# The gate projection of the first block: from 24 plain weight panels to 42 half-size block products

## The chip, the cores and the metric

One core of a Trainium2 chip runs the whole program. The metric is the device time of one execution in microseconds; each kernel is run several times and the median is quoted. The engines are TensorE (PE, matmuls, with its weight loads as PEld), VectorE (DVE), ScalarE (ACT), GpSimd (POOL) and SyncE (SP, which issues most of the DMA transfers). They run side by side, each through its own list of instructions in order, and meet at semaphores.

## The reference

The program computes two transformer blocks on 512 tokens of 1024 features, in fp32. The change touches only the gates of the first block:

```
h = rmsnorm(x, attn_norm_g[l])
z = h @ w_in[l]
gates = jax.nn.sigmoid(h @ w_gate[l] + b_gate[l])
...
merged = g_a * (y_a @ proj_a[l]) + g_b * (y_b @ proj_b[l]) + g_c * (y_c @ proj_c[l])
x = x + merged @ w_out[l]
```

`w_gate` is 1024 x 3072, so the gates are one product of 512 x 1024 by 1024 x 3072. Beside it stands the attention of four heads, `y_c`: for each head two score matrices of 512 x 512 (causal), a softmax of each, their difference, and the product with the values. The gates are first used when the branches `y_a`, `y_b`, `y_c` are projected and merged.

## The kernel before, in words

Activations lie feature by feature: a tile of 128 features by 512 tokens. Every fp32 product is made of three matmuls (`three`): the high part of the weights by the high part of x, high by low, low by high. A **panel** is 128 x 1024 weights, that is, all eight 128 x 128 blocks that one tile of 128 output features needs; it costs 24 matmuls of 512 columns. Panels come by a ring of four: SP loads one into `stage` (a place is free again when DVE has made the low part of the panel four earlier), ACT copies it into the high part `wh` (`hi`; it waits for the load, and for PE to have finished the panel four earlier), DVE subtracts to the low part `wl` (`lo`), and PE multiplies (`features`), then raises `panel_done`.

The order of work is written out by hand for each engine. The stages around the change: u, va, pool (18 panels are numbered up to the gates, `P_GATE` = 18), then eight panels of queries and keys (`P_Q`), the spatial and pool products, four panels of values (`P_V`), then 24 gate panels, then `P_PROJ`, `P_WOUT` and the feed-forward `P_UP`.

The first 16 gate panels are spread over the four heads, four to a head, in a hardware loop `Fori(0, 4)`. In one head PE does: gate panel 0; scores of query blocks 0 and 1; panel 1 with scores 2 and 3 in its middle; panel 2; panel 3 with the transposes of the softmax (`turn`) between its parts; then the product with the values (`values`). DVE takes each gate panel from PSUM and scales it by the row norm (`evac_row` into `tmp`), takes bias and maximum of the score blocks (`score_pair`, L1486), blends the two softmaxes (L1523 to L1532), and makes low parts. ACT makes the high parts, the tanh of the gates, the exponentials (`exp_pair`) and the high part of the transposed softmax. The last eight gate panels stand beside the norms of the four head outputs: sums of squares (`head_sums`, `turn_heads`), a power on POOL, a row spread over the partitions (`head_row`), and the high and low parts of `yc`, on which the projection waits (`yc_ready`).

POOL is nearly idle here. Later, in the two feed-forwards, the same seven-product scheme is already in use: sums of weight blocks are made by DMA transfers that add into SBUF (`add_first1`, L1964, and `add_third1`, L1971), and by DVE.

Of the kernel before, what the change touches and what calls it, by code (L numbers as in the profile page):

```python
# [54 lines left out]
P_U, P_VA, P_POOL, P_Q, P_K, P_V, P_GATE, P_PROJ, P_WOUT, P_UP = 0, 2, 4, 6, 10, 14, 18, 42, 50, 58  # L55
# [223 lines left out]
def semaphores(nc):  # L279
# [457 lines left out]
def sync_program(nc, sp, s, b, dram, scratch, out):  # L737
# [46 lines left out]
    for row in range(P_UP // RING * RING, P_UP):  # L784
        load_row(row, row - RING)
# [44 lines left out]
    for u in range(RING):  # L830
        sp.dma_start(b.stage[:, (start + u) % RING, :], stream[start + u]).then_inc(s.load[(start + u) % RING], 16)
# [59 lines left out]
def scalar_program(nc, act, s, b, dram, scratch, line_dram, out):  # L891
# [97 lines left out]
    def gate(g, half, dst, evac):  # L989
        act.wait_ge(s.evac, evac + 1)  # L990
        bias = b.half_bg[:, g:g + 1] if isinstance(g, int) else b.half_bg[:, bass.ds(g, 1)]
        AR(dst, b.tmp[:, half, :], ACT.Tanh, bias=bias, scale=0.5).then_inc(s.gated, 1)
# [8 lines left out]
    with act.Fori(0, 4) as i:  # L1001

        act.dma_start(b.bias[:], bias_tile(scratch, i)).then_inc(s.bias_in, 16)
        act.wait_ge(s.evac, E_K + 4)
        AR(b.qh[:], b.qk[:, i, :], ACT.Copy, scale=0.125).then_inc(s.qk_hi, 1)
        AR(b.kh[:], b.qk[:, 4 + i, :], ACT.Copy).then_inc(s.qk_hi, 1)
        act.wait_ge(s.evac, E_V + 4)
        AR(b.vh[:], b.v[:, :, bass.ds(P * i, P)], ACT.Copy).then_inc(s.v_hi, 1)
        for u in range(4):
            hi(Panel(P_GATE + u + RING, RING, i))  # L1010
            if u != 2:
                gate(4 * i + u, u % 2, b.ga[:, 4 * i + u, :], E_GATE + 4 * i + u)
            if u == 0:
                for qb in range(TT):
                    act.wait_ge(s.negated, 4 * i + qb + 1)
                    exp_pair(qb)
            if u == 2:
                for kb in range(TT):
                    if kb == 2:
                        gate(4 * i + u, u % 2, b.ga[:, 4 * i + u, :], E_GATE + 4 * i + u)  # L1020
                    act.wait_ge(s.turned, 4 * i + kb + 1)
                    w = (TT - kb) * P
                    A(b.th[:, turned_offset(kb):turned_offset(kb) + w], b.ps[:, 5 + kb % 2, 0:w],
                      ACT.Copy).then_inc(s.turned_hi, 1)

        act.wait_ge(s.scored, 8 * i + 8)
        act.wait_ge(s.score_done, 8 * i + 8)
        act.wait_ge(s.pv_done, i + 1)


    act.wait_ge(s.pv_done, 4)
    for pair in range(2):
# [6 lines left out]
    for u in range(8):  # L1039
        hi(Panel(P_GATE + 16 + u + RING))  # L1040
        gate(16 + u, u % 2, b.gatec[:, u, :], E_GATE + 16 + u)
        if u == 0:
            act.wait_ge(s.ocol_done, 1)
            A(b.osum[0:4, :], b.ps[0:4, 7, :], ACT.Copy).then_inc(s.o_squared, 1)
        if u == 1:
# [3 lines left out]
        if 3 <= u < 7:  # L1049
            h = u - 3  # L1050
            act.wait_ge(s.o_normed, h + 1)
            A(b.ych[:, h, :], b.o[:, h, :], ACT.Copy, scale=b.subln).then_inc(s.yc_hi, 1)
# [256 lines left out]
def vector_program(nc, dve, s, b):  # L1309
# [2774 lines left out]
```

## Time and profile before

| | us |
|---|---|
| median of three runs | 1427.68 (1427.46 to 1429.75) |
| the profiled execution | 1428.33 |
| its span in the trace | 1426.6 |
| PE busy | 1415.9 (99% of the span) |
| DVE busy | 1084.4 (76%) |
| ACT busy | 756.8 (53%) |
| POOL busy | 71.9 (5%) |
| DMA | 198.64 MB, mean 139 GB/s |

The profiled execution lasted 1.7 us longer than its span, which is what lies around the traced instructions. The clock granted to PE is full in all 40 slices of the page. Matmuls overlap in the trace: the length shown for one is more than the distance to the next, so a stretch of PE is measured from start to start. Times in the timeline are microseconds from the start of the span.

### The profile page before, as it was taken

Reading aid. Unit: us, or ns where it says so; the run is one execution under the profiler, and the core shown is the slowest. Engines: PE = TensorE matmul, PEld = TensorE weight load, DVE = VectorE, ACT = ScalarE, POOL = GpSimd, SP = SyncE. Lnnn points to the kernel's source line nnn. Section 1 sums busy time; section 2 is a strip of 40 time slices with the busy share of each in tenths; the row PEclk is TensorE's granted clock in tenths of the full one; section 3 lists DMA queues with packets and bytes.
Section 4 is the critical chain, followed back from the end, with each engine's and each line's share of the span. In section 5 each row is a group of like instructions: output and inputs, shape, how many; then the busy total and the mean of one; then the engine's idle time right before and its main releaser. Section 6 shows DMA issues by size and latency. Waiting matters only on the chain.

```text
span 1426.6 us, 22475 instructions
## 1 busy us (share of the span) xinstructions
PE 1415.9 (99%) x8561; PEld 1235.3 (87%) x8561; DVE 1084.4 (76%) x1591; ACT 756.8 (53%) x1071; POOL 71.9 (5%) x81
## 2 busy tenths in 40 slices
PE   9999999999999999999999999999999999999997
PEld 7878888888899999999988777878888989899896
DVE  4836675686899699879857776967655897979888
ACT  6215555334666465456734555535434866657474
POOL 0000000000100000000000000000000100000100
PEclk9999999999999999999999999999999999999999
DMA  8722222233556776765243323213212867585851
GB/s 297 244 87 89 92 72 89 89 94 102 174 163 160 223 175 175 198 184 136 79 160 103 117 92 118 75 62 119 72 45 73 242 178 211 151 240 133 241 142 74
DMA packets 56573, 198.64 MB, mean 139 GB/s; under 512 B 6136, under 2 KB 6648, under 8 KB 56228
## 3 DMA queue, kind: packets, MB, share of 16 engines
q1 hardware_dynamic: 43584, 155.47, 32.8%
q0 software_dynamic: 8640, 30.94, 12.2%
q10 hardware_dynamic: 4260, 11.00, 2.4%
q8 instruction: 61, 1.00, 0.3%
q14 instruction: 28, 0.23, 0.1%
HBM read 195.26 MB, written 6.06 MB: 141 GB/s over the span
## 4 chain that ended last, share of the span: by engine, by line
PE 94%; DVE 3%; DMA 1%; issue 1%; ACT 0%; SPq 0%; POOLq 0%; POOL 0%; DVEq 0%; ACTq 0%
PE ps L2045 30%; PE ps L2047 29%; PE ps L2046 29%; PE ps L2209 1%; DMA raw_sum<-down_dram 1%; PE ps L2224 1%; PE ps L3676 1%; PE ps L3576 1%; DVE wl L1642 1%; PE ps L2097 0%; DMA tables<-tables_dram 0%; DVE y L3369 0%; DVE xcl L1774 0%; PE ps L3696 0%; DVE raw_sum L1649 0%
## 5 line engine op out<-in xcount | busy, mean ns | idle before, releaser
L2046 PE MATMUL ps<-hl,wh 128*128 128x512 f32 (+1 forms) x1024 | 351.4, 343 | 0.0
L2045 PE MATMUL ps<-hh,wh 128*128 128x512 f32 (+1 forms) x952 | 337.4, 354 | 0.0
L2047 PE MATMUL ps<-hh,wl 128*128 128x512 f32 (+1 forms) x952 | 331.2, 348 | 0.0
L908 ACT ACTIVATE wh<-stage 128x1024 fp32r<-128x1024 f32 x129 | 136.2, 1058 | 255.2 <-PE ps L2047 247.0
L2046 PEld LDWEIGHTS ps<-hl,wh 128*128 128x128 f32 x1024 | 194.4, 190 | 19.9
L2045 PEld LDWEIGHTS ps<-hh,wh 128*128 128x128 f32 x952 | 180.4, 189 | 26.8 <-issue 4.3
L2047 PEld LDWEIGHTS ps<-hh,wl 128*128 128x128 f32 x952 | 180.3, 189 | 23.4
L1324 DVE TENSOR_TENSOR wl<-stage,wh 128x1024 fp32r<-128x1024 f32 x128 | 156.1, 1221 | 49.1 <-ACT wh L908 48.9
L3256 DVE TENSOR_TENSOR wl<-raw,wh 128x1024 fp32r<-128x1024 f32 x75 | 90.9, 1220 | 20.6 <-ACT wh L2664 20.4
L1642 DVE TENSOR_TENSOR wl<-raw,wh 128x1024 fp32r<-128x1024 f32 (+1 forms) x75 | 88.7, 1187 | 22.4 <-ACT wh L1103 21.9
L2664 ACT ACTIVATE wh<-raw 128x1024 fp32r<-128x1024 f32 x75 | 78.7, 1054 | 50.8 <-PE ps L2047 45.0
L1103 ACT ACTIVATE wh<-raw 128x1024 fp32r<-128x1024 f32 (+1 forms) x75 | 76.5, 1026 | 49.1 <-PE ps L2047 43.6
L2045 PE MATMUL ps<-xch,wh 128*128 128x256 f32 x308 | 87.5, 284 | 0.8 <-DVE wl L1642 0.5
L2045 PE MATMUL ps<-wh,xch 128*128 128x512 f32 x224 | 87.2, 389 | 0.0
L2046 PE MATMUL ps<-wl,xch 128*128 128x512 f32 x224 | 87.2, 389 | 0.0
L2046 PE MATMUL ps<-xcl,wh 128*128 128x256 f32 x308 | 87.2, 283 | 0.0
L2047 PE MATMUL ps<-xch,wl 128*128 128x256 f32 x308 | 87.1, 283 | 0.0
L2047 PE MATMUL ps<-wh,xcl 128*128 128x512 f32 x224 | 87.1, 389 | 0.0
L2045 PE MATMUL ps<-sums_hi,wh 128*128 128x256 f32 x288 | 81.5, 283 | 0.0
L2047 PE MATMUL ps<-sums_hi,wl 128*128 128x256 f32 x288 | 81.5, 283 | 0.0
L2045 PE MATMUL ps<-xsh,wh 128*128 128x256 f32 x224 | 63.4, 283 | 0.0
L2046 PE MATMUL ps<-xsl,wh 128*128 128x256 f32 x224 | 63.4, 283 | 0.0
(475 smaller groups left out, 3239.9 us busy)
## 6 DMA issues: line engine op xcount, KB each, us to landing
stage<-stream_dram SPq DMA_DIRECT2D x134, 512.0 KB, 3.6
raw<-up_dram SPq DMA_DIRECT2D x64, 512.0 KB, 7.1
raw<-down_dram SPq DMA_DIRECT2D x52, 512.0 KB, 5.9
raw_sum<-up_dram SPq DMA_DIRECT2D x16, 512.0 KB, 3.9
raw_sum<-up_dram POOLq DMA_DIRECT2D x16, 512.0 KB, 8.3
raw<-up_dram POOLq DMA_DIRECT2D x16, 512.0 KB, 8.9
raw_sum<-down_dram SPq DMA_DIRECT2D x13, 512.0 KB, 4.7
raw_sum<-down_dram POOLq DMA_DIRECT2D x13, 512.0 KB, 7.8
```

The source lines that it names most:

```text
L908: A(parts_of(b, p)[0], b.stage[:, p.stage, :], ACT.Copy).then_inc(s.hi_ready, 1)
L1103: A(b.wh[:, p.slot, 0:p.width], weight_block1(b, p), ACT.Copy).then_inc(s.hi_ready, 1)
L1324: V.tensor_tensor(wl, b.stage[:, p.stage, :], f32(wh), ALU.subtract).then_inc(s.lo_ready, 1)
L1642: V.tensor_tensor(b.wl[:, p.slot, 0:p.width], weight_block1(b, p), f32(b.wh[:, p.slot, 0:p.width]), ALU.subtract).then_inc(s.lo_ready, 1)
L2045: MM(out, wh, xh, start=start, stop=False, skip_group_check=True)
L2046: MM(out, wh, xl, start=False, stop=False, skip_group_check=True)
L2047: return MM(out, wl, xh, start=False, stop=stop, skip_group_check=True)
L2209: ins = MM(b.ps[:, 4 + 2 * (qb % 2) + c, 0:width], q[part, tok], k[part, 0:width], start=n == 0, stop=n == 2, skip_group_check=True)
L2224: ins = nc.tensor.transpose(b.ps[:, 5 + kb % 2, P * (qb - kb):P * (qb - kb) + P], b.s[:, c, at:at + P], b.ident)
L2664: A(b.wh[:, p.slot, :], weight_block(b, p), ACT.Copy).then_inc(s.hi_ready, 1)
L3256: V.tensor_tensor(b.wl[:, p.slot, :], weight_block(b, p), f32(b.wh[:, p.slot, :]), ALU.subtract).then_inc(s.lo_ready, 1)
L3576: ins = MM(b.ps[half, 7, kb * P:T], b.vp[:, kb, half], b.turned[:, c, at:at + width], start=kb == 0, stop=kb == TT - 1, skip_group_check=True)
```

## The change

The gate weights no longer come as 24 panels of the stream. They are cut into six groups of 512 output features (four tiles of 128). For a group the kernel makes the 512 x 512 result as a 2 x 2 block product by Winograd's form of Strassen's scheme: seven products of half-size blocks in place of eight. The order of a group is `ORDER1` = P1, Q5, P6, Q3, P7, P2, R4. Each of the seven has one panel of 128 x 1024 weights, and costs 24 matmuls of 256 columns.

- **Weights.** Four of the seven need sums or differences of weight blocks. POOL makes them in DRAM, in a new tensor `gate_sums`: it copies a block from `gates`, waits, adds another with an accumulating transfer, waits, copies the sum, and so on. For a pair of groups there are 16 transfers in six dependent steps (`SUM_LEVEL`: panels Q5 and P7 are there after 8 transfers, P6 after 12, R4 after 16). There are three pairs. SP waits for the sum before it loads its panel.
- **x.** Between the query and the value panels ACT scales x by the norm gain (8 instructions), DVE scales it by the row norm and forms sums, and both split seven blocks in high and low parts (`gx`). Some of them lie where x, `hh` and `hl` were, so x is loaded again from DRAM after the gates.
- **PSUM.** A group holds three banks (`GATE_BANKS`). P1 is copied by ACT to the bank of P2 (`gate_seed`); the states of Q5's and P6's banks are copied to `diag` (`gate_copy`); DVE makes the two difference halves (`gate_sub`, after Q3 and after P7) and ACT takes tanh of these and, straight from PSUM, of the two other halves (`gate_bank`, `gate_differences`).
- **Order.** The loop over heads is unrolled. A head now stands beside one group: scores 0 and 1 in P6, scores 2 and 3 in Q3, transposes in R4, and the product with the values in P1 of the next group. Groups 4 and 5 stand beside the head norms.
- Before R4, PE waits for both `gate_sub` of the group (`s.evac` at `E_GATE + 4 * g + 4`), because R4 goes on into the bank that `gate_sub` reads.

The core of the diff, numbering and SP first:

```diff
-P_U, P_VA, P_POOL, P_Q, P_K, P_V, P_GATE, P_PROJ, P_WOUT, P_UP = 0, 2, 4, 6, 10, 14, 18, 42, 50, 58
+GATE_GROUPS = 6
+GATE_ITEMS = 7 * GATE_GROUPS
...
+GATE_SUM = {Q5: 0, P6: 1, R4: 2, P7: 3}
+GATE_BLOCK = {P1: 0, Q3: 2, P2: 3}
+SUM_LEVEL = {Q5: 8, P7: 8, P6: 12, R4: 16}
...
+    for row in range(P_GATE, P_PROJ):
+        g, product = gate_item(row)
+        if product in GATE_SUM:
+            sp.wait_ge(s.gate_sums.sem, s.gate_sums.at(256 * (g // 2) + 16 * SUM_LEVEL[product]))
+            source = dram["gate_sums"][g, GATE_SUM[product]]
+        else:
+            source = dram["gates"][g, GATE_BLOCK[product]]
+        sp.wait_ge(s.lo_ready, row - RING + 1)
+        sp.dma_start(b.stage[:, row % RING, :], source).then_inc(s.load[row % RING], 16)
```

ACT, one head:

```diff
+    for i in range(4):
+        first = gate_panel(i, P1).index + RING
...
+        gate_seed(i)
...
+        hi(Panel(first))
+        gate_copy(i, Q5)
+        hi(Panel(first + 1))
...
+        exps(i, 0)
+        exps(i, 1)
+        gate_copy(i, P6)
+        hi(Panel(first + 2))
...
+        exps(i, 2)
+        exps(i, 3)
+        hi(Panel(first + 3))
+        hi(Panel(first + 4))
+        gate_bank(i, P2)
+        hi(Panel(first + 5))
+        gate_differences(i)
+        turned(i, range(TT))
+        hi(Panel(first + 6))
+        gate_bank(i, R4)
```

DVE:

```diff
+    for i in range(4):
...
+        lo(Panel(first + 1))
+        score_pair(i, 1, 0, (b.bias, b.bias))
...
+        lo(Panel(first + 2))
+        for qb in (2, 3):
+            score_pair(i, qb, 0, (b.bias, b.bias))
...
+        gate_sub(i, Q3)
+        blend(i)
+        gate_sub(i, P7)
+        lo(Panel(first + 3))
+        lo(Panel(first + 4))
+        turned_rest(i, (0, 1))
+        lo(Panel(first + 5))
+        turned_rest(i, (2, 3))
+        lo(Panel(first + 6))
```

POOL:

```diff
+    for pair in range(GATE_GROUPS // 2):
+        groups = (2 * pair, 2 * pair + 1)
+        if pair:
+            summed(16 * pair)
+        for g in groups:
+            copied(g, 0, dram["gates"][g, 0])
+            copied(g, 3, dram["gates"][g, 1])
+        summed(16 * pair + 4)
+        for g in groups:
+            added(g, 0, 1)
+            added(g, 3, 2)
+        summed(16 * pair + 8)
+        for g in groups:
+            copied(g, 1, dram["gate_sums"][g, 0])
+        summed(16 * pair + 10)
+        for g in groups:
+            added(g, 1, 2)
+        summed(16 * pair + 12)
+        for g in groups:
+            copied(g, 2, dram["gate_sums"][g, 1])
+        summed(16 * pair + 14)
+        for g in groups:
+            added(g, 2, 3)
```

PE, for one product of one group:

```diff
+        elif product == R4:
+            pe.wait_ge(s.evac, E_GATE + 4 * g + 4)
+        high, low = b.gx[GATE_X[product]]
+        for m in range(PAIRS2):
+            for n in range(2):
+                for step in between.get(2 * m + n, ()):
+                    step()
+                wh, wl = w(p, M * m + P * n)
+                ins = three(b.ps[:, bank, M * n:M * n + M], wh, wl, high[:, m, :], low[:, m, :],
+                            product in (P1, Q5) and m == 0 and n == 0, m == PAIRS2 - 1)
+        ins.then_inc(s.panel_done, 1)
```

Where the work stands now shows best in DVE's list. Before, from the scores of query block 1 to the end of the blend in one head; `s,mx<-ps,bias` takes bias and maximum of a score block, `rec` begins the blend, `wl<-stage,wh` is a low part of a panel, `tmp<-ps,rrow` a gate panel taken from PSUM:

```order
L1324 TENSOR_TENSOR wl<-stage,wh 128x1024
...
L1493 ISA s,mx<-ps,bias 128x256
...
L1493 ISA s,mx<-ps,bias 128x384
...
L1493 ISA s,mx<-ps,bias 128x512
...
L1497 TENSOR_SCALAR neg<-mx 128x2
...
L1329 TENSOR_TENSOR tmp<-ps,rrow 128x512
L1523 RECIPROCAL rec<-sums 128x4
```

After, the same stretch of the second head; `tmp<-ps,diag` and `tmp<-diag,ps` are the two `gate_sub`:

```order
L1719 ISA s,mx<-ps,bias 128x256
...
L1484 TENSOR_TENSOR wl<-stage,wh 128x1024
...
L1719 ISA s,mx<-ps,bias 128x384
...
L1719 ISA s,mx<-ps,bias 128x512
...
L1704 TENSOR_TENSOR tmp<-ps,diag 128x2x256
L1738 RECIPROCAL rec<-sums 128x4
...
L1747 SCALAR_TENSOR_TENSOR s<-s,rec 128x512
L1708 TENSOR_TENSOR tmp<-diag,ps 128x2x256
L1484 TENSOR_TENSOR wl<-stage,wh 128x1024 x2
```

Now a low part of a panel stands between the scores of block 1 and those of blocks 2 and 3, and the second `gate_sub`, on which R4 waits, stands behind the whole blend.

ACT's list of one head before; `wh<-stage` is a high part of a panel, `s,sums<-s,neg` an exponential, `ga<-tmp` the tanh of a gate panel:

```order
L908 ACTIVATE wh<-stage 128x1024
...
L898 ACTIVATE ga<-tmp,half_bg 128x512
...
L999 ACTIVATE s,sums<-s,neg 128x128 x2
...
L999 ACTIVATE s,sums<-s,neg 128x256 x2
...
L999 ACTIVATE s,sums<-s,neg 128x384 x2
...
L999 ACTIVATE s,sums<-s,neg 128x512 x2
...
L908 ACTIVATE wh<-stage 128x1024
```

And after; `diag<-ps` are the copies of Q5's and P6's banks:

```order
L1096 ACTIVATE diag<-ps 128x512
L966 ACTIVATE wh<-stage 128x1024
L1121 ACTIVATE s,sums<-s,neg 128x128 x2
L1121 ACTIVATE s,sums<-s,neg 128x256 x2
L1096 ACTIVATE diag<-ps 128x512
L966 ACTIVATE wh<-stage 128x1024
L1121 ACTIVATE s,sums<-s,neg 128x384 x2
L1121 ACTIVATE s,sums<-s,neg 128x512 x2
L966 ACTIVATE wh<-stage 128x1024 x2
L956 ACTIVATE ga<-ps,half_bg 128x256 x2
L966 ACTIVATE wh<-stage 128x1024
L956 ACTIVATE ga<-tmp,half_bg 128x512 x2
```

Between the exponentials of blocks 1 and 2 stand a copy that waits for the end of P6, and a high part.

## Rows read from the trace of the kernel before

**Rows 1.** The page: busy time by engine, and the chain that ended last by engine.
```profile
PE 1415.9 (99%) x8561; PEld 1235.3 (87%) x8561; DVE 1084.4 (76%) x1591; ACT 756.8 (53%) x1071; POOL 71.9 (5%) x81
...
PE 94%; DVE 3%; DMA 1%; issue 1%; ACT 0%; SPq 0%; POOLq 0%; POOL 0%; DVEq 0%; ACTq 0%
```

**Rows 2.** Windows: stretch, length; busy PE, PEld, DVE, ACT, POOL (x); clock, DMA share, GB/s.
```profile
112.76:270.92 158.16, 158.16 (x789) 127.83 (x788) 103.54 (x253) 80.90 (x156) 2.90 (x1) 1.00 0.27 86
112.76:140.13 27.37, 27.37 (x143) 22.15 (x142) 20.07 (x56) 15.53 (x32) 0.00 (x0) 1.00 0.27 87
```

**Rows 3.** PE timeline: start us, us, engine line op out<-in; second head's first panel.
```profile
138.26 0.39 PE L2045 MATMUL ps<-th,vh 128*128 128x512 f32 x1
...
140.12 0.44 PE L2045 MATMUL ps<-hh,wh 128*128 128x512 f32 x1
...
140.86 0.39 PE L2045 MATMUL ps<-hh,wh 128*128 128x512 f32 x1
...
144.94 0.39 PE L2045 MATMUL ps<-hh,wh 128*128 128x512 f32 x1
```

**Rows 4.** Chain of waits: start us, us; first head's score products.
```profile
118.18 0.89 PE ps L2209 x12
...
122.02 1.42 PE ps L2209 x12
```

**Rows 5.** PE timeline: 256-column products of the first feed-forward.
```profile
402.92 0.28 PE L2045 MATMUL ps<-x11h,wh 128*128 128x256 f32 x1
...
405.79 0.28 PE L2045 MATMUL ps<-sums_hi,wh 128*128 128x256 f32 x1
```

**Rows 6.** DVE timeline of the first head.
```profile
119.48 1.23 DVE L1324 TENSOR_TENSOR wl<-stage,wh 128x1024 fp32r<-128x1024 f32 x1
...
120.64 0.42 DVE L1493 CUSTOM_DVE_ANT_0 s<-ps,bias 128x256 f32<-128x256 f32 x1
...
122.78 0.55 DVE L1493 CUSTOM_DVE_ANT_0 s<-ps,bias 128x384 f32<-128x384 f32 x1 [1.16 <-issue]
...
124.04 0.69 DVE L1493 CUSTOM_DVE_ANT_0 s<-ps,bias 128x512 f32<-128x512 f32 x1
...
125.39 0.17 DVE L1497 TENSOR_SCALAR neg<-mx 128x2 f32<-128x2 f32 x1
...
127.15 0.18 DVE L1523 RECIPROCAL rec<-sums 128x4 f32<-128x4 f32 x1
...
130.88 1.22 DVE L1324 TENSOR_TENSOR wl<-stage,wh 128x1024 fp32r<-128x1024 f32 x1
```

**Rows 7.** ACT timeline of the first head.
```profile
121.65 0.51 ACT L999 ACTIVATE s<-s,neg 128x256 f32<-128x256 f32 x1 [0.99 <-DVE neg L1497]
...
122.56 0.19 ACT L999 ACTIVATION_READ_ACCUMULATOR s<-s,neg 128x1 f32 x1
...
125.59 0.72 ACT L999 ACTIVATE s<-s,neg 128x512 f32<-128x512 f32 x1 [0.21 <-DVE neg L1497]
...
127.02 1.04 ACT L908 ACTIVATE wh<-stage 128x1024 fp32r<-128x1024 f32 x1
```

**Rows 8.** Groups by line, ACT, first feed-forward: busy us, mean ns | idle.
```profile
L1149 ACT ACTIVATE diag<-ps 128x512 f32<-128x512 f32 x14 | 8.4, 598 | 8.8 <-PE ps L2047 8.8
```

**Rows 9.** ACT timeline: four high parts of 512 in a row.
```profile
238.24 2.18 ACT L1048 ACTIVATE yabh<-yab 128x512 fp32r<-128x512 f32 x4
```

**Rows 10.** POOL timeline: the last instruction ahead of the place of the sums.
```profile
43.89 1.02 POOL L1952 TENSOR_TENSOR small<-small 128x4 f32<-128x4 f32 x1 [12.21 <-DVE small L1408]
```

**Rows 11.** DMA issues, KB, median us to landing: one add, two adds, gate stage loads.
```profile
raw_sum<-up_dram POOLq DMA_DIRECT2D x1, 512.0 KB, 5.7
...
raw<-up_dram POOLq DMA_DIRECT2D x2, 512.0 KB, 6.6
...
stage<-stream_dram SPq DMA_DIRECT2D x24, 512.0 KB, 3.6
```

**Rows 12.** DMA queue, 56 to 60 us: packets, MB, share; a DRAM-to-DRAM copy runs alone.
```profile
q10 hardware_dynamic: 486, 1.24, 77.5%
```

More of the change, by code:

```diff
@@ L666, in evacs1, with gate_panel, gate_item, stream_row @@
     return E_UP + PLAIN1 + 4 * number
+GATE_BANKS = (0, 1, 2), (3, 2, 1)
+GATE_X = {P1: "X11", Q5: "S1", P6: "S2", Q3: "Q3", P7: "S3", P2: "X12", R4: "X22"}
+GX_ACT = (*(f"gain{k}" for k in range(KT)), "X11", "S1", "S2", "X12 moved", "X22 moved", "Q3", "S3", "X12", "X22")
+GX_DVE = ("D0", "D1", "S1", "X22", "X11", "X12", "S2", "X11 rest", "S1 rest", "S2 rest", "Q3", "S3",
+          "Q3 rest", "S3 rest", "X12 rest", "X22 rest")
+GATE_SUM = {Q5: 0, P6: 1, R4: 2, P7: 3}
+GATE_BLOCK = {P1: 0, Q3: 2, P2: 3}
+SUM_LEVEL = {Q5: 8, P7: 8, P6: 12, R4: 16}
+def gate_panel(g, product):
+    return Panel(P_GATE + 7 * g + ORDER1.index(product))
+def gate_item(row):
+    g, n = divmod(row - P_GATE, 7)
+    return g, ORDER1[n]
+def stream_row(row):
+    return row - GATE_ITEMS if row >= P_PROJ else row
 XN_READY = ("X11T", "X12", "S1", "X22", "S2", "Q3", "S3")
@@ L782, in block1 @@
         sp.dma_start(b.raw1[:, r, p.half, 0:p.width], weights1(dram, p, r)).then_inc(s.block_in1[p.half][r].sem, 16)
-    for row in range(P_UP // RING * RING, P_UP):
+    for row in range(P_PROJ + 2 * RING, P_UP):
         load_row(row, row - RING)
@@ L983, in scalar_program, with gate_tile @@
+    for u in range(2 * RING):
+        hi(Panel(P_Q + u + RING))
+        if u < RING:
+            gate_gain(2 * u)
+            gate_gain(2 * u + 1)
+        elif u == 6:
+            gate_hi("X11")
+        elif u == 7:
+            gate_hi("S1")
     for u in range(4):
         hi(Panel(P_V + u + RING))
+        if u == 0:
+            gate_hi("S2")
+            gate_move("X12")
+            gate_move("X22")
     act.wait_ge(s.lines_out, 32)
[L989 to L992, printed above, removed]
+    def gate_tile(n):
+        return b.ga[:, n, :] if n < 16 else b.gatec[:, n - 16, :]
@@ new lines, in tanh, with gate_bank, gate_differences @@
+    def tanh(dst, source, n):
+        return AR(dst, source, ACT.Tanh, bias=b.half_bg[:, n:n + 1], scale=0.5)
+    def gate_bank(g, product):
+        bank_b, bank_a, _ = GATE_BANKS[g % 2]
+        bank, h = (bank_a, 1) if product == P2 else (bank_b, 0)
+        act.wait_ge(s.panel_done, gate_panel(g, product).index + 1)
+        for n in range(2):
+            ins = tanh(gate_tile(4 * g + n)[:, M * h:M * h + M], b.ps[:, bank, M * n:M * n + M], 4 * g + n)
+        ins.then_inc(s.gated, 1)
+    def gate_differences(g):
+        act.wait_ge(s.evac, E_GATE + 4 * g + 4)
+        for n in range(2):
+            tanh(gate_tile(4 * g + 2 + n), b.tmp[:, n, :], 4 * g + 2 + n).then_inc(s.gated, 1)
@@ L999, in exp_pair, with squares @@
             A(sc, sc, ACT.Exp, bias=b.neg[:, n:n + 1], accum_out=b.sums[:, n:n + 1]).then_inc(s.exped, 1)
[L1001 to L1032, printed above, removed]
+    def squares(pair):
         for h in (2 * pair, 2 * pair + 1):
@@ L1048, in scalar_program @@
                 A(b.yabh[:, k, :], b.yab[:, k, :], ACT.Copy).then_inc(s.yab_hi, 1)
[L1049 to L1052, printed above, removed]
+        hi(Panel(first + 1))
+        gate_copy(g, P6)
+        hi(Panel(first + 2))
+        hi(Panel(first + 3))
+        if g == 4:
+            act.wait_ge(s.ocol_done, 1)
+            A(b.osum[0:4, :], b.ps[0:4, 7, :], ACT.Copy).then_inc(s.o_squared, 1)
+        hi(Panel(first + 4))
+        gate_bank(g, P2)
+        hi(Panel(first + 5))
+        gate_differences(g)
+        if g == 5:
+            for h in range(4):
+                act.wait_ge(s.o_normed, h + 1)
+                A(b.ych[:, h, :], b.o[:, h, :], ACT.Copy, scale=b.subln).then_inc(s.yc_hi, 1)
+        hi(Panel(first + 6))
+        gate_bank(g, R4)
     act.wait_ge(s.yab_ready, 4)
```

436 lines of the change are left out of this document (316 added, 120 removed).

## The prediction

> **What bounds the kernel now.** I read the page first: PE is busy 99% of the span, DVE 76%, ACT 53%, and the chain that ended last is 94% PE [rows 1]. So time is saved only where PE has less to do, and lost wherever PE comes to wait. Then the windows of the gate stage: 158.2 us with PE busy all of it, clock 1.00, DVE 103.5, ACT 80.9, DMA share 0.27; in the first head 27.37 us with DVE at 20.07 and ACT at 15.53 [rows 2]. Nothing waits there, but DVE has only a quarter of slack. Then the PE timeline for the distance between matmuls: six triples of 512 columns from 140.86 to 144.94, 0.680 a triple, so a gate panel costs 8 x 0.68 = 5.44 [rows 3]; eight triples of 256 columns from 402.92 to 405.79, 0.359 a triple, so a block product costs 2.87 [rows 5]. Last the DVE, ACT and DMA rows, for the lengths of what PE may come to wait for.
>
> **PE's own work.** Removed: 24 panels x 5.44 = 130.6. Added: 42 products x 2.87 = 120.5. PE saves 10.1; I take 9.6, since each of the seven products starts with one slower matmul somewhere. The other 27.6 of the stage (scores 0.89 and 1.42 a head [rows 4], value product 1.86 [rows 3], transposes, head norms) stay. This gain, 1.6 a group, is all there is; everything below is against it.
>
> **A head's chain of work (the main term).** A group with a head has 20.1 of products, and DVE now makes seven low parts of 1.16 (119.48 to 120.64 [rows 6]) where it made four. I lay out one head (groups 1 to 3) from the start of its P1 at 0. PE alone: P1 with the value product to 4.7; Q5 to 7.6; P6 with scores 0.89 to 11.4; Q3 with scores 1.42 to 15.7; P7 to 18.6; P2 to 21.5. R4 could start at 21.6, but it waits for the second `gate_sub`, which stands behind the blend on DVE. Backwards from the scores:
> - P1 done 4.7; ACT seeds (0.6 [rows 8]), high part of v, high part of a panel (0.95 of pitch, record 1.04 [rows 7]): 6.9. DVE low part 8.05, v 8.7, score pair 0 (scores there at 8.5) 9.3, low part 10.5, score pair 1 (0.9) 11.4.
> - ACT exponentials of block 1, 121.65 to 122.75 = 1.1 [rows 7]: 12.5. Only then the copy of P6 (0.6 [rows 8]) 13.1, high part 14.1; DVE low part 15.25.
> - Score pair 2, 122.78 to 124.04 = 1.26: 16.5; score pair 3, 124.04 to 125.56 = 1.52: 18.0 [rows 6]. Exponentials of block 3, 125.59 to 127.12 = 1.53: 19.6 [rows 7]. Blend, 127.15 to 130.88 = 3.73: 23.3 [rows 6]. `gate_sub`, at 0.65: 24.0.
>
> So PE waits from 21.6 to 24.0. The third transpose, in R4's middle, waits for a low part of the transposed softmax, and ahead of that on DVE stand two panel low parts (26.35) and itself (26.95), where PE is there at 26.3: 0.6 more. 3.0 a head, 9.0 for three heads; the head ends at about 28.7, against 27.4 to 27.6 before. Group 0 has four more blocks of x on ACT and DVE: X12 and X22 lie between the score pairs and before the blend, each some 1.0 to 1.2 on the chain, while its P1 has no value product: I lay it out to 4.5. Heads together: 13.5. Bounds: if each of these estimates is 0.25 kinder per step (eight steps) the wait is 1 a head (4 in all); if pitch is the full record length, 5 a head (20).
>
> **The end of the stage.** The projection waits for `yc_ready`. Before, heads were finished one by one between panels. Now ACT has, from P7 of group 5 at 0: P2 done 2.9, tanh of two halves 0.9, high part 1.0, two tanh 1.25, then four high parts of `yc` in a row (2.18 for four [rows 9]) = 8.3, and DVE's last low part 0.7: 9.0, where PE would start at 5.8. 3.2, taken as 3.0 (0 to 5).
>
> **x blocks, copies, reload.** ACT gets 8 scalings of 512, 7 high parts and 2 moves of 1024 (about 13), DVE about 18, between 49 and 118 us. The panel rhythm there is 5.44 with DVE at 1.85 to 3 of it, so they lie beside PE: 0 (up to +2 if one lands in group 0's chain later than I lay it). The reload of x, 2 MB ahead of nothing urgent, and the unrolled loops: 0 (−0.5 to +1).
>
> **The sums in DRAM.** POOL is free after 44.9 [rows 10]. No row shows an add into DRAM; the nearest are adds into SBUF: one lands after 5.7, and of two issued together the median is 6.6, so a further add costs 1.8 to 2.7 more [rows 11]. I take 2.6. A copy from DRAM to DRAM runs at 1.24 MB in 4 us, so 1.7 a block [rows 12], with 2.4 fixed (a load of 512 KB lands in 3.6 [rows 11]). Four copies 9.2, four adds 13.5, then twice two copies 5.8 and two adds 8.3: 51 a pair alone, of which 16 are fixed. Loads share the engines: 28 transfers filled 0.27 of them [rows 2], 46 in about the same time some 0.43, of which I let two thirds fall on the sums: 16 + 35/0.72 = 65 a pair. The first pair also meets the bias copy until 61 and ends near 114; pair 1 has its P6 sums (12 transfers) at 161 and ends at 179; pair 2 has them at 226. ACT wants P6 of group 2 during R4 of group 1, so the sum by 159.5, and P6 of group 4 by 217. It stands in line there ahead of the tanh and of the transposed softmax, so being late stops R4: 1.5, then 7 more with the first taken off: I take 7 in all. Bounds: 0 if a pair takes 57 or less; with 80 a pair (adds at 3.3, copies at 2.5) the sums set the pace and cost 35.
>
> The page "DMA: Bandwidth & Descriptors" of the Trainium skill (Anatomy of one DMA) fits 2.0 us + bytes/436e3 per transfer from POOL, 3.2 for a block; an add here took 5.7, so the trace doesn't bear that out for adds. By that rule a pair would take an estimated 31, and this term would be 0.
>
> **Sum.** 1428.3 (profiled execution) − 9.6 + 13.5 + 3.0 + 7 = 1442.2. The median of the runs lies 0.6 below that execution, so 1441.6; I say 1442.
>
> **The rivals.**
> - *Sums in time.* The heads' chain and the end alone: 1428.3 − 9.6 + 16.5 = 1435. For it: the pair needs only 57, against 51 alone. Against: the loads become 42.
> - *The sums set the pace.* As above with 80 a pair: 1435 + 35 = 1470; at 72, about 1455. For it: adds beside loads, and adds whose target is DRAM, which no row prices. Against: a single add is at 5.7.
> - *PE doesn't wait (faster).* One mechanism: the exponentials of block 1 end before P6 does, and the second `gate_sub` comes before P2 ends. That needs the way from P6's end (11.4) to `gate_sub` in 10.2, where I count 12.6; then only the 9.6 are left, less 3 at the end or less: 1419 to 1422. For it: DVE would be at some 22 of 26. Against: eight dependent steps with measured lengths. It decides at 1.3 a head, where gain and wait are even.
> - *Even.* Half of the chain's wait and no late sums: 1427 to 1430.
>
> **Chances.** Forecast with sums somewhat late (1437 to 1450) 0.40; sums in time but heads waiting (1431 to 1437) 0.25; sums set the pace (over 1450) 0.14; even 0.09; faster 0.12. A change of 0.2% (2.9 us) is what a measurement of this kernel can tell from none. So faster 0.12, same 0.10, slower 0.78. The range leaves out the faster case and the upper half of the pace case: 1428 to 1462.
>
> **What would show it.** In the changed profile: 24 matmuls of 256 columns in 2.87; PE idle ahead of R4's first matmul, ended by DVE's `tmp<-diag,ps`, 2 to 3 in each of heads 1 to 3 and 4 in head 0; PE idle ahead of the projection, ended by `ycl`; ACT idle for a `stage` load from `gate_sums`, or SP waiting for POOL, ahead of group 2 and group 4; POOL's 16 transfers a pair in 60 to 70. Wrong would be: heads shorter than 27.4, a pair over 75 or under 57, or waits in the query and value stages. A gate stage shorter than 158 means that the chain of a head is not as I laid it.

## The result: 1465.5 us, slower by 2.6%

The changed kernel takes 1465.49 us (median of 4 runs, 1464.01 to 1466.86), the kernel before 1427.61 beside it: ratio 1.0262, 95% interval 1.0244 to 1.0279. The prediction said 1442, with a range of 1428 to 1462. The sign was right and the time was not: it lies in the rival "the sums set the pace" (1455 at 72 us for the sums of a pair of groups, 1470 at 80). The profiled execution took 1465.08, with a span of 1462.6 against 1426.6.

The page after, to be read beside [rows 1]: busy time by engine, the granted clock in 40 slices, the chain that ended last by engine and by line.

```profile
PE 1416.9 (97%) x8993; PEld 1259.7 (86%) x8993; DVE 1113.6 (76%) x1613; ACT 796.9 (54%) x1136; POOL 104.0 (7%) x129
...
PEclk9999898999999999999999999999999999999999
...
PE 82%; DMA 9%; issue 5%; DVE 2%; POOL 1%; ACT 1%; SPq 0%; POOLq 0%; DVEq 0%; ACTq 0%
PE ps L2356 26%; PE ps L2357 25%; PE ps L2358 25%; DMA gate_sums<-gates_dram 6%; DMA gate_sums<-gate_sums 2%; PE ps L4025 1%; POOL gate_sums L2238 1%; PE ps L2520 1%; PE ps L2535 1%; PE ps L3925 1%; POOL gate_sums L2235 0%; PE ps L2408 0%; DMA tables<-tables_dram 0%; DVE y L3718 0%; PE ps L4045 0%
```

The chain was 94% PE; now 8% of it is transfers into `gate_sums`. PE has less work to do and yet is busy 1.0 us longer: part of its time runs at a lower clock. Where the time went is shown by windows (stretch, length; busy PE, PEld, DVE, ACT, POOL; clock, DMA share, GB/s): the gate stage, first product to projection, then stretches of it, to be read against [rows 2].

```profile
112.17:304.93 192.76, 156.81 (x1221) 150.50 (x1220) 121.36 (x265) 112.87 (x209) 24.63 (x33) 0.91 0.76 216
112.00:140.00 28.00, 24.70 (x195) 23.68 (x194) 25.02 (x58) 21.59 (x40) 3.79 (x6) 0.94 0.88 257
...
170.00:200.00 30.00, 21.34 (x156) 20.39 (x157) 13.48 (x39) 14.18 (x29) 4.68 (x8) 0.77 0.86 264
...
230.00:260.00 30.00, 16.28 (x114) 15.77 (x113) 13.72 (x27) 12.70 (x25) 4.42 (x6) 0.77 0.73 176
260.00:290.00 30.00, 30.00 (x247) 28.74 (x246) 16.15 (x20) 19.39 (x31) 2.92 (x1) 1.00 0.53 176
```

The stage has 192.8 in place of 158.2: 34.6 of the span's 36.0. PE stands idle for 192.76 − 156.81 = 36.0 of it. The waits of the stage (engine, operation, line, who released it: us in total, times, longest), between 100 and 330:

```profile
ACT wh L966 <- DMA stage<-gate_sums: 25.6, 5, 11.7
...
PE ps L2535 <- DVE tl L1754: 22.5, 2, 11.6
...
PE ps L2356 <- DVE tmp L1708: 9.7, 4, 3.3
...
PE ps L2356 <- issue: 3.8, 1, 3.8
```

22.5 + 9.7 + 3.8 = 36.0, all of PE's idle time. The four waits of 9.7 stand ahead of R4 and the 3.8 ahead of the projection, as the prediction placed them. The two of 22.5 are ahead of the third transposed block of groups 1 and 3. How a late sum gets there is read from ACT's timeline around the first (start us, us, operation, idle before it and its releaser):

```profile
160.65 1.99 ACT L966 ACTIVATE wh<-stage 128x1024 fp32r<-128x1024 f32 x2
163.23 0.84 ACT L956 ACTIVATE ga<-ps,half_bg 128x256 f32<-128x256 f32 x2 [0.59 <-PE ps L2358]
175.12 1.06 ACT L966 ACTIVATE wh<-stage 128x1024 fp32r<-128x1024 f32 x1 [11.05 <-DMA stage<-gate_sums]
176.08 1.32 ACT L956 ACTIVATE ga<-tmp,half_bg 128x512 f32<-128x512 f32 x2
177.31 0.95 ACT L1135 ACTIVATE th<-ps 128x512 fp32r<-128x512 f32 x2
```

ACT is free at 164.07 (175.12 less 11.05) and stands for the panel of group 2's P6 until 175.12; the tanh and the turned softmax, whose inputs were there by 165.2 and 166.7, come behind it. What PE does after such a wait is in its timeline and in windows of 4 us:

```profile
112.17 0.28 PE L2356 MATMUL ps<-gx_X,wh 128*128 128x256 f32 x1
...
115.04 0.28 PE L2356 MATMUL ps<-gx_S,wh 128*128 128x256 f32 x1
...
178.66 0.69 PE L2535 MATMUL ps<-consts,s 128*128 128x128 f32 x2 [10.91 <-DVE tl L1754]
...
181.28 0.41 PE L2356 MATMUL ps<-gx_X,wh 128*128 128x256 f32 x1
```

```profile
178.60:182.60 4.00, 3.94 (x19) 3.94 (x20) 2.23 (x5) 1.04 (x3) 0.84 (x1) 0.50 1.04 249
182.60:186.60 4.00, 4.00 (x26) 3.87 (x26) 2.75 (x4) 2.45 (x5) 0.83 (x1) 0.83 0.61 152
186.60:190.60 4.00, 4.00 (x35) 3.87 (x35) 1.11 (x2) 2.06 (x3) 0.00 (x0) 1.00 0.98 131
```

A product costs what was predicted (112.17 to 115.04 = 2.87, as in [rows 5]). After 10.91 idle the granted clock is 0.50 (1.2 of 2.4 GHz), and 19 matmuls fit into 4 us, then 26, then 35: about 25 matmuls of 0.115 are missing, some 2.9 us that no wait shows. By the lengths of its matmuls PE is at the lower clock until 183.8, 5.2 us.

Last, the sums. POOL's timeline, the first pair and the second:

```profile
44.45 2.41 POOL L2235 DMA_DIRECT2D gate_sums<-gates_dram  x4
57.09 2.55 POOL L2238 DMA_DIRECT2D gate_sums<-gates_dram  x3 [10.22 <-DMA gate_sums<-gates_dram]
75.79 0.83 POOL L2238 DMA_DIRECT2D gate_sums<-gates_dram  x1 [16.15 <-issue]
84.37 1.02 POOL L2235 DMA_DIRECT2D gate_sums<-gate_sums  x2 [7.75 <-DMA gate_sums<-gates_dram]
...
120.05 1.97 POOL L2235 DMA_DIRECT2D gate_sums<-gates_dram  x4 [8.16 <-DMA gate_sums<-gates_dram]
...
171.76 1.02 POOL L2235 DMA_DIRECT2D gate_sums<-gate_sums  x2 [7.33 <-DMA gate_sums<-gates_dram]
...
191.50 1.99 POOL L2235 DMA_DIRECT2D gate_sums<-gates_dram  x4 [5.46 <-DMA gate_sums<-gates_dram]
```

A pair takes 120.05 − 44.45 = 75.6, then 71.5, where 65 was predicted. The four adds of the first take 27.3 (57.09 to 84.37), the four copies ahead of them 12.6. POOL issues three adds and then stands for 16.15 with nothing but "issue" named: there are 56.3 us of that in 7 places. That stop is not always after three adds: at 90.91 it comes after one, at 204.77 after two. The P6 sums of pair 1 are there at 171.8 (predicted 161), of pair 2 at 243.9 (predicted 226).

### The profile page after: what moved, and what is told of

The parts are those of the page before. It is cut to its first block, busy times and chain, and to the rows that moved or that the text cites. A ratio compares the mean times of both kernels' runs of the same rounds, so it can differ in the third digit from the quotient of the medians.

```text
span 1462.6 us, 23129 instructions
## 1 busy us (share of the span) xinstructions
PE 1416.9 (97%) x8993; PEld 1259.7 (86%) x8993; DVE 1113.6 (76%) x1613; ACT 796.9 (54%) x1136; POOL 104.0 (7%) x129
## 4 chain that ended last, share of the span: by engine, by line
PE 82%; DMA 9%; issue 5%; DVE 2%; POOL 1%; ACT 1%; SPq 0%; POOLq 0%; DVEq 0%; ACTq 0%
PE ps L2356 26%; PE ps L2357 25%; PE ps L2358 25%; DMA gate_sums<-gates_dram 6%; DMA gate_sums<-gate_sums 2%; PE ps L4025 1%; POOL gate_sums L2238 1%; PE ps L2520 1%; PE ps L2535 1%; PE ps L3925 1%; POOL gate_sums L2235 0%; PE ps L2408 0%; DMA tables<-tables_dram 0%; DVE y L3718 0%; PE ps L4045 0%
## 5 line engine op out<-in xcount | busy, mean ns | idle before, releaser
L966 ACT ACTIVATE wh<-stage 128x1024 fp32r<-128x1024 f32 x147 | 154.8, 1056 | 236.6 <-PE ps L2358 202.4
L2357 PE MATMUL ps<-hl,wh 128*128 128x256 f32 (+1 forms) x832 | 276.5, 332 | 0.0
L2356 PE MATMUL ps<-hh,wh 128*128 128x512 f32 (+1 forms) x760 | 260.0, 342 | 0.1
L2358 PE MATMUL ps<-hh,wl 128*128 128x512 f32 (+1 forms) x760 | 256.3, 337 | 0.0
L1484 DVE TENSOR_TENSOR wl<-stage,wh 128x1024 fp32r<-128x1024 f32 x146 | 177.7, 1221 | 72.5 <-ACT wh L966 72.4
L2357 PEld LDWEIGHTS ps<-hl,wh 128*128 128x128 f32 x832 | 158.2, 190 | 13.5
L2356 PEld LDWEIGHTS ps<-hh,wh 128*128 128x128 f32 x760 | 144.3, 190 | 17.9 <-issue 2.9
L2358 PEld LDWEIGHTS ps<-hh,wl 128*128 128x128 f32 x760 | 144.3, 190 | 15.5
L1919 DVE TENSOR_TENSOR wl<-raw,wh 128x1024 fp32r<-128x1024 f32 (+1 forms) x75 | 88.7, 1186 | 22.4 <-ACT wh L1263 21.8
```

What stands on the lines that cost most here:

```text
L966: A(parts_of(b, p)[0], b.stage[:, p.stage, :], ACT.Copy).then_inc(s.hi_ready, 1)
L1484: V.tensor_tensor(wl, b.stage[:, p.stage, :], f32(wh), ALU.subtract).then_inc(s.lo_ready, 1)
L1919: V.tensor_tensor(b.wl[:, p.slot, 0:p.width], weight_block1(b, p), f32(b.wh[:, p.slot, 0:p.width]), ALU.subtract).then_inc(s.lo_ready, 1)
L2356: MM(out, wh, xh, start=start, stop=False, skip_group_check=True)
L2357: MM(out, wh, xl, start=False, stop=False, skip_group_check=True)
L2358: return MM(out, wl, xh, start=False, stop=stop, skip_group_check=True)
```

## The experiments

The kernels without real sums compute something other than the gates; they are there for their time. Theory A: the extra time is late sums plus the chain of work in a head, the end of the stage, and the low clock behind each wait. Times are medians beside the kernel before at 1428.0 to 1428.8.

**Without sums.** POOL's loop over the pairs is empty, and the loads take plain blocks.

```
-            sp.wait_ge(s.gate_sums.sem, ...)
-            source = dram["gate_sums"][g, GATE_SUM[product]]
+            source = dram["gates"][g, GATE_SUM[product]]
...
-    for pair in range(GATE_GROUPS // 2):
+    for pair in ():
```

> This kernel makes no weight sums: GpSimd issues none of its 48 transfers, and the loads of the gate stage take plain blocks of the weights without waiting (the weight sums are left out of what is computed). Theory A (the sums are late, the head's chain and the clock do the rest): the time falls from 1465 to 1428.3 - 9.6 (products) + 9.7 (four waits ahead of R4) + 3.8 (ahead of the projection) + 4 to 8 (matmuls at half clock behind those waits) = 1436 to 1441; the two waits of 11 us ahead of the turned softmax are gone, the ones ahead of R4 stay at 2 to 3 each. Rival B (the sums are not the matter, the wait for the turned softmax comes from the order of the head's work on ScalarE and VectorE): 1455 or more, the 11 us waits stay. Rival C (the head's waits too come from the transfers): 1419 to 1430.

1438.01, ratio 1.0067 (1.0051 to 1.0084): as theory A has it. The 22.5 are gone, 9.7 and 3.8 stay. So the sums cost 1465.5 − 1438.0 = 27.5, the largest part by far. Its stage, beside that of the last kernel below that has neither wait:

```profile
112.07:278.44 166.37, 152.22 (x1222) 145.92 (x1220) 120.73 (x265) 113.17 (x209) 2.90 (x1) 0.98 0.44 140
```
```profile
112.04:261.56 149.52, 148.81 (x1221) 142.60 (x1220) 118.89 (x264) 111.19 (x208) 2.90 (x1) 1.00 0.47 152
```

The same matmuls keep PE busy 152.2 at clock 0.98 and 148.8 at 1.00: 3.4 of low clock within the stage, on 14.2 of idle time against 0.7.

**Sums made, not waited for.** The first part of the same edit alone; POOL keeps its 48 transfers, and the loads take plain blocks.

> GpSimd makes all weight sums as before, with its 48 transfers, but no load waits for them or takes them: the gate stage loads plain blocks (so its products use blocks in place of sums). Theory A (only being late costs): as the kernel without sums, within 2 us, 1436 to 1442. Rival D (the transfers crowd the DMA engines, busy over 0.8 of the time, so that plain loads come late too): 1448 to 1465, with ScalarE idle for loads of plain blocks.

1446.08, ratio 1.0118 (1.0101 to 1.0135): between the two. Plain loads of the stage now land after 5.9 in place of 3.3, yet no wait of PE leads back to them. Of the 8.1 more than without sums, 6.9 are one wait:

```profile
263.42 1.11 PE L2407 MATMUL ps<-consts,small 128*128 128x128 f32 x4 [6.89 <-POOL small L2264]
```

POOL computes the power for the heads' norms behind its last adds (258.69 to 260.41), and the quicker stage gets there sooner than the sums end. So what the transfers cost here is a place in POOL's queue, not late loads: neither PE nor ACT has a wait on a load in the stage. No view splits the remaining 1.2.

**Copies in place of adds.**

```
-        G.dma_start(dram["gate_sums"][g, n], dram["gates"][g, r], accum_op=ALU.add,
-                    max_dma_last_dim=4 * D).then_inc(...)
+        G.dma_start(dram["gate_sums"][g, n], dram["gates"][g, r]).then_inc(...)
```

> The 24 adding transfers into DRAM are plain copies in the same places, all waits kept (so the sums hold a block in place of a sum). Theory A1 (the adding, and its 128 rows where a copy has 16, is what is slow: 7.7 us against some 5): a chain of a pair falls from 72 to about 50 us, the sums are in time, 1437 to 1443. Rival A2 (the number of dependent transfers and the traffic between DRAM and DRAM set the pace, not the adding): a pair stays at 65 to 72 us and the time at 1455 to 1465.

1440.88, ratio 1.0087 (1.0070 to 1.0104), which is 2.9 above the kernel without sums by the medians; its profiled execution (1437.62) was its quickest and has the waits of the kernel without sums. A pair takes 98.73 − 44.32 = 54.4 and then 47.9:

```profile
44.32 2.42 POOL L2235 DMA_DIRECT2D gate_sums<-gates_dram  x4
56.03 1.93 POOL L2238 DMA_DIRECT2D gate_sums<-gates_dram  x4 [9.30 <-DMA gate_sums<-gates_dram]
68.99 0.97 POOL L2235 DMA_DIRECT2D gate_sums<-gate_sums  x2 [11.03 <-DMA gate_sums<-gates_dram]
```

So the number of dependent transfers alone does not make the sums late. What does is the adding, or its rows: an add goes in 128 rows, a copy in 16, and this edit changes both.

**Adds in longer and in shorter rows.** `max_dma_last_dim=8 * D` (64 rows of 8 KB), and `2 * D` (256 rows of 2 KB).

> The adds go in 64 rows of 8 KB in place of 128 rows of 4 KB; nothing else is changed, and all that the kernel computes stays. Theory R (GpSimd can't issue the next add before room for its rows is free, which shows as its waits of 16 us in all ended by nothing but issue): twice as many adds are under way at once, the waits on issue go, a pair falls from 72 to 60 us or less and the time to 1440 to 1450. Rival E (the DMA engines themselves are full while they add, whatever the rows): a pair stays within 3 us and the time at 1460 to 1467.

> The changed kernel with each add in 256 rows of 2 KB in place of 128 of 4 KB; nothing else is changed. Theory R (what limits GpSimd's adds is room for their rows, three adds of 128 rows at once, four of 64): now one add of 256 rows at a time, the waits ended by nothing but issue grow from 56 in 7 to over 80 in more than 12 places, a pair takes over 80 us and the time is over 1475. Rival E (the engines' rate of adding is what limits, rows don't matter): waits on issue as before, a pair 68 to 76, the time 1460 to 1470.

Long rows 1453.81, ratio 1.0178 (1.0156 to 1.0200); short rows 1489.45, ratio 1.0419 (1.0401 to 1.0437). Short rows are as theory R has it in all it says: 99.5 us of waits on issue in 15 places, pairs of 87.7 and 80.5. Long rows go its way and not its length: the time is 3.8 above its range, the pairs take 70.0 and 68.0 in place of 60, and waits on issue stay. The start of the first pair in each, long rows ahead:

```profile
57.01 3.25 POOL L2238 DMA_DIRECT2D gate_sums<-gates_dram  x4 [10.23 <-DMA gate_sums<-gates_dram]
77.92 1.03 POOL L2235 DMA_DIRECT2D gate_sums<-gate_sums  x2 [17.66 <-DMA gate_sums<-gates_dram]
```
```profile
57.20 0.94 POOL L2238 DMA_DIRECT2D gate_sums<-gates_dram  x1 [10.54 <-DMA gate_sums<-gates_dram]
69.01 0.91 POOL L2238 DMA_DIRECT2D gate_sums<-gates_dram  x1 [10.87 <-issue]
80.31 0.88 POOL L2238 DMA_DIRECT2D gate_sums<-gates_dram  x1 [10.39 <-issue]
86.73 0.90 POOL L2238 DMA_DIRECT2D gate_sums<-gates_dram  x1 [5.54 <-issue]
93.42 1.02 POOL L2235 DMA_DIRECT2D gate_sums<-gate_sums  x2 [5.79 <-DMA gate_sums<-gates_dram]
```

In the first pair POOL has out at once four adds of 64 rows, three of 128, one of 256; its waits on issue are 30.3, 56.3 and 99.5 us over all pairs. The four adds of the first pair take 20.9, 27.3, 36.2, those of the second 21.6, 25.7, 31.2, those of the third 21.7, 20.7, 27.7; four copies in their place take 13.0, 9.6, 9.7. So rows of 2 KB always cost more, and 64 rows in place of 128 help in two pairs of three. What the engines do meanwhile is in the pages: POOL's own queue, its packets, MB and share of the 16 engines' span, without sums, with copies only, with adds in 64, 128 and 256 rows:

```profile
q0 software_dynamic: 8640, 30.94, 12.1%
```
```profile
q0 software_dynamic: 10176, 56.11, 16.9%
```
```profile
q0 software_dynamic: 11328, 56.11, 19.1%
```
```profile
q0 software_dynamic: 12864, 56.11, 19.3%
```
```profile
q0 software_dynamic: 15936, 56.11, 19.7%
```

Each share times its span, less the first: the 48 transfers fill the engines for 69, 103, 109 and 119 us. That is 1.4 a copy, and 2.9, 3.1 and 3.5 an add. The packets bear out the rows, 16 more than rows each: 32 for a copy, 80, 144 and 272 for an add. So there are two costs. An add holds the engines twice as long as a copy of the same bytes (no run has adds and copies in equally many rows, so the 2.9 can hold a part for its 64 rows). And POOL stops at the issue, the more so the more rows there are. With long rows the engines are busy for 0.99 of the first four adds, so little is left there for a further gain; with short rows for 0.78. I expected a pair of 60 with long rows since I saw only the second cost, and it did not go altogether.

The Trainium skill bears on both. "Collectives: The Full Stack" (The bandwidth ceiling) says of the add in a reduce-scatter that it reads two sources and emits two read descriptors where a copy emits one; the 2.9 against 1.4 here agrees with that. "DMA: Bandwidth & Descriptors" (SWDGE vs HWDGE vs iDMA) says that descriptors of GpSimd's transfers are written to rings in SBUF. That POOL stops sooner with more rows agrees with a ring that fills up; that it also stops after one add of 64 rows (at 85.62 with long rows, 4.93 of wait) is not explained by the count of rows, and no run here changed the size of a ring.

**The late panel behind the softmax.** In groups 0 to 3, on ACT (and likewise on DVE):

```
         gate_bank(i, P2)
-        hi(Panel(first + 5))
         gate_differences(i)
         turned(i, range(TT))
+        hi(Panel(first + 5))
```

> The changed kernel with one thing moved: in groups 0 to 3 ScalarE's high part and VectorE's low part of the panel of P6 of the next group come behind the turned softmax, not ahead of it. The sums come as late as before. Theory A (a late sum costs because the turned softmax stands behind it in line): ScalarE now waits for the sum with the turned softmax done, some 4 us later in the group; of the two waits of 11 us PE keeps only what the sum is late for P6 itself, about 4 to 7 each; the time falls from 1465 to 1450 to 1458. Rival (what the sums cost is their lateness for the product and no more, wherever the wait stands): within 3 us of 1465.

1458.00, ratio 1.0218 (1.0201 to 1.0235): 7.5 less than the changed kernel, at the upper edge of what was expected. The 22.5 became 0.7, with 3.6 more ahead of R4, 4.2 ahead of scores and 4.1 at a seed. The place in line nearly doubled the waiting for late sums (22.5 against 12.6). In time it is less: the sums cost 20.0 here (1458.0 − 1438.0) and 27.5 before. These 20.0 are the lateness itself, the other 7.5 the place in line.

**The head's order**, on top of the kernel without sums and with the late panel behind the softmax (shortened; DVE's low parts and `turned_rest` move along):

```
+        for qb in (2, 3): score_pair(i, qb, ...)
         lo(Panel(first + 2))
-        for qb in (2, 3): score_pair(i, qb, ...)
...
     blend: four scalings by rec
+        gate_sub(i, P7)
     blend: four sums
-        gate_sub(i, P7)
...
-   R4: {1: [tn(g, 0), tn(g, 1)], 4: [tn(g, 2)], 6: [tn(g, 3)]}   P1: {4: [pv(g - 1)]}
+   R4: {4: [tn(g, 0), tn(g, 1)], 7: [tn(g, 2)]}   P1: {1: [tn(g - 1, 3)], 6: [pv(g - 1)]}
```

> On top of the kernel without sums and with the panel of P6 moved: the second gate_sub stands inside the blend, ahead of its second half; VectorE makes the low part of the third panel behind the score pairs of blocks 2 and 3, not ahead; the four turned blocks come later on TensorE (in R4 at 4 and 7, the last and the value product in the next P1). Theory A (the path from P6 over copy, low part, score pairs, exponentials and blend to the second gate_sub holds R4): the four waits of 9.7 in all fall to 0 to 3, the half clock behind them goes too, and the time falls from 1438 to 1425 to 1430. Rival (the head is bound by VectorE's or ScalarE's whole work, and the wait shows elsewhere, ahead of the turned blocks or of the next scores): 1435 to 1439, with waits of the same sum in other places.

1424.48, ratio 0.9973 (0.9962 to 0.9983): the four waits ahead of R4 are gone (0.2 of waiting is left in the heads), and 13.5 us with them: by the pages PE's idle time falls by 10.6 and its busy time, at the better clock, by 2.3. Theory A, slightly past its range.

**The end's order**, also on the kernel without sums: on ACT the four `ych` come ahead of the panel before `gate_bank(g, P2)`, on DVE the four `ycl` ahead of `gate_lo(5)`.

> On top of the kernel without sums: in group 5 the high and low parts of yc come ahead of the tanh of P2, not behind the last two tanh. Theory A (the projection waits for the parts of yc, 3.8, and then runs some 14 matmuls at half clock, 3 more): the wait goes, 1438 to 1431 to 1434. Rival (the gate tanh themselves, or the last panels, are as late): 1436 to 1438.

1433.47, ratio 1.0034 (1.0021 to 1.0047): 4.5 less. The projection's first matmul waits 0.20 in place of 3.76. As expected.

**Both orders without sums**, the late panel behind the softmax among them. This is the floor.

> Without the weight sums (plain blocks loaded in their place), with both orders, the head's and the end's: what is left when the sums cost nothing. Theory A (products save 9.6 and nothing else is left against it but a wait or two under 1 us): 1424.5 - 4.5 = 1418 to 1421. Rival (head and end share a cost, the clock behind a wait): 1422 to 1425.

1418.75, ratio 0.9933 (0.9920 to 0.9947). The kernel before ran beside it at 1428.41: 9.66 less, which is the predicted saving of the products, 9.6. Its stage is the second row of the pair above. So on balance nothing else in the change costs time: not the x blocks, the copies, the reload nor the unrolled loops.

**All of it with real sums:** long rows, late panel, both orders.

> The whole computation: the changed kernel with the adds in rows of 8 KB, the panel of P6 behind the turned softmax, the head's order and the end's order as in the two kernels before. Theory A: the terms add up; 1454 - 10 to 13 (late sums no longer hold the softmax) - 8 to 11 (head) - 4 to 7 (end) = 1423 to 1432, so about even with the kernel before, or faster by up to 5. Rival (with the head quicker, the sums, at 66 to 70 us a pair, are late again for the quicker head): 1435 to 1445.

1445.37, ratio 1.0124 (1.0107 to 1.0141). The sum of terms failed, the rival was right (0.4 past its upper end): a quicker head meets the same late sums. Its waits in the stage:

```profile
PE ps L2356 <- ACT ps L1089: 12.1, 1, 12.1
...
PE ps L2520 <- DVE o L1733: 7.8, 1, 7.8
```

**Pairs overlapped; then also begun earlier.** The next pair's first copies and adds go out with this pair's last ones, each of two neighbouring pairs on a semaphore of its own (shortened):

```
         for g in groups(pair):
             copied(g, 2, dram["gate_sums"][g, 1])
+        if pair < 2: firsts(pair + 1)
         summed(pair, 14)
         for g in groups(pair):
             added(g, 2, 3)
+        if pair < 2: first_adds(pair + 1)
```

> The whole computation, on top of the kernel with long rows and the head's and the end's order (1445): the sums of the next pair begin while those of this pair still run. With the last two copies of a pair go the four first copies of the next, with its last two adds the next pair's four first adds; each of two neighbouring pairs has its own semaphore. Theory A (the chain of dependent transfers with gaps between them, not the engines' full capacity, sets how late a sum is): a pair takes some 54 in place of 66 us, P6's sum of pair 1 is there at about 145 to 155 (was 166) and of pair 2 at 200 to 215 (was 240); the waits of 7.8 and 12.1 go; 1421 to 1430. Rival (the DMA engines are full, at 0.8 to 1.0 of the time, and overlap only shifts the waits): 1436 to 1446.

> The same, with the first four copies issued ahead of GpSimd's power for the layer norm, at about 32 in place of 44 us. Theory A: all sums some 8 to 12 us sooner; 1420 to 1428, and not above the kernel before it by more than 2 unless the copies delay the loads of the query and key stage, where TensorE would show waits before 112 us (rival: 1428 to 1435).

Overlapped: 1431.44, ratio 1.0016 (1.0004 to 1.0028), 13.9 below the kernel just above, 1.4 past the upper end expected; pair 1 has its P6 sums at 153.6, pair 2 at 210.6. Begun earlier as well: 1426.06, ratio 0.9979 (0.9970 to 0.9988), with P6 sums at 138.3 and 198.2. **It is the one version with the whole computation that beats both kernels**, by 0.2% the one before and by 39 us the changed one. PE shows no new wait before 112. It is 7.3 above the floor. 4.5 of that is one wait, at 182.45, and ahead of it the DMA engines are full: a share of 0.97 from 140 to 170 and of 1.03 from 168 to 180, and a plain load issued at 168.54 serves ACT at 179.38.

```profile
140.00:170.00 30.00, 29.38 (x239) 27.83 (x239) 24.26 (x60) 21.40 (x46) 6.76 (x10) 1.00 0.97 297
```
```profile
179.38 1.06 ACT L967 ACTIVATE wh<-stage 128x1024 fp32r<-128x1024 f32 x1 [4.10 <-DMA stage<-gates_dram]
```

## Why the prediction was wrong, step by step

- **Products, −9.6: right.** −9.66 with everything else taken away.
- **The heads' chain, +13.5: the place right, the total right by luck.** Predicted were waits of 4.5 in group 0 and 2.4 for R4 in each other group; measured 3.3 and 2.1 (9.7 in all), with 0.7 in place of 1.8 for the third transpose. Undoing it gave 13.5, since what I had too much in waits came back as low clock, which I had not priced. The place I laid out is the right one: R4, behind the second `gate_sub`. The run that removed the wait moved the whole path at once and other things with it (the late panel, the transposes and the value product on PE), so no link of the path is shown by itself.
- **The end, +3.0: the wait right, its price low.** 3.8 of waiting, worth 4.5 to 5.7 with its clock (1438.0 − 1433.5; 1424.5 − 1418.75).
- **x blocks, copies, reload, 0: right**, by the floor.
- **The sums, +7: this step failed.** It is mis-sized: 27.5. Three things in it:
  - *A pair.* 65 was said, 75.6, 71.5 and some 68 came. The work of the engines was near: 35 of the 51 were to be theirs, and the pages give 109/3 = 36 (a copy less than I said, an add more). The time around it was not. By my sum, with the fixed part left whole (2.4 in a step of copies, 3.1 in one of adds) and the rest over 0.72, the six steps of a pair are 11.8, 17.5, 7.1, 10.3, 7.1, 10.3; the first pair took 12.6, 27.3, 6.5, 12.0, 7.3, 9.9, the second 10.8, 25.7, 6.2, 9.1, 7.1, 12.6. So nearly all of the excess is the four adds issued together, 9.8 and 8.2. For these POOL stood at the issue (16.15, and 7.02 and 8.28), which I had no row for; with 64 rows in place of 128, 6.4 and 4.0 of it went. The rest stays in part open. In the first pair the engines are full, with a share of 1.00 from 57.09 to 75.79: the bias copy, all but over by 61 in the kernel before, still takes 14 to 28% of them up to 81 here, and I had counted only the loads beside the sums.
  - *From pair to wait.* My own rule, P6's sum late by so much and ACT standing in line, then gives the rest: with the sums at 171.8 in place of 161, the first wait is 1.5 + 10.8 = 12.3; ACT stood 11.05. With those of pair 2 at 243.9 it gives 243.9 − 217 = 26.9 for both; 22.5 of PE's waiting came. The rival at 72 us a pair said 20 for the sums. So the mechanism was right, and the chance of 0.14 was too low for a chain whose four adds no row priced.
  - *The clock, not counted at all.* The stage is 26.4 longer than without sums (192.76 against 166.37): 21.8 of it PE stands idle, and 4.6 it is busy longer on the same products (156.81 against 152.22), at the lower clock behind the waits. The whole changed kernel lies 45.9 above the floor's span: PE idle 34.4 longer, and busy 11.5 longer (1416.9 against 1405.4) on the same 8993 matmuls.
- **The terms by these runs:** 1428.3 − 9.6 + 13.5 + 5.7 + 27.5 = 1465.4. That it meets the measured 1465.1 proves nothing, since each term is the difference of two neighbouring runs; it shows the sizes.
- "DMA: Bandwidth & Descriptors" of the Trainium skill, as quoted ahead of the result, gives 3.2 for a block. The estimate of 31 a pair worked out from it is too low for adds (68 to 76) and for copies alone as well (48 to 54), both with the loads beside them.

## What to carry to other kernels

Work moved to an engine that is idle, here POOL and the DMA engines, is free only while its whole dependent chain keeps ahead of the first reader; price each link by a row of its own kind, and where there is none, put the chance on the dear side. Where a load may be late, put its reader behind all other work that is ready on that engine, and look at what else stands in the producer's queue. And price a wait of TensorE at more than its length: here 10 us of waiting cost 12 to 13.

## What the runs showed of the hardware

- Adds from DRAM into DRAM: in the first pair four of 512 KB together take 20.9 (64 rows each), 27.3 (128) or 36.2 (256), copies of the same blocks 13.0. An add holds the engines for 2.9, 3.1 and 3.5 us of their time, a copy for 1.4. POOL can stand at the issue of the next one: for 30, 56 and 99 us in all, after four, three or one in the first pair and sometimes after fewer.
- The granted clock fell to 0.50 for some 5 us behind waits of 10.9 and 11.6, and also behind short ones: in the window behind the wait of 3.3 ahead of the first R4 it is 0.59, behind the 3.8 ahead of the projection 0.50. Behind the wait of 2.14 at 207.0 it is 0.61: PE first runs on at full clock, its products of 256 columns last 0.41 in place of 0.28 from 208.7, and are back at 0.28 at 211.4. Behind the two of 2.13 at 165.3 and 236.7 it is 1.00, but there PE worked for 2.4 us only before it stood again; what tells these apart stays open.

```profile
304.90:308.90 4.00, 3.97 (x9) 3.14 (x10) 1.09 (x1) 0.55 (x2) 0.00 (x0) 0.50 0.42 132
...
135.50:139.50 4.00, 3.93 (x22) 3.96 (x22) 3.73 (x5) 2.81 (x5) 0.62 (x1) 0.59 0.71 167
```

- A high DMA share did not by itself hold up a reader: in the run with sums made and not waited for it is 0.82 to 0.96 in the windows of 30 us from 140 to 260, and neither PE nor ACT waits for a load. At 1.03 over 12 us, in the last kernel, ACT did.
